# Sparse attention: ScalarE takes the next exponentials and the output copy ahead of a stored gate's silu, and the weight split after it

## The reference, cut to what matters

```python
logits = jnp.einsum('bqcgd,bqncd->bqcgn', qb, k_sel).astype(jnp.float32)
logits = logits + bias.astype(jnp.float32)
logits = jnp.where(valid[:, :, None, None, :], logits, -1e30)
p = jax.nn.softmax(logits, axis=-1).astype(v.dtype)
o = jnp.einsum('bqcgn,bqncd->bqcgd', p, v_sel)
...
o = o.transpose(1, 0, 2, 3).reshape(B, L, DSA_HEADS * DSA_HD)
return o * jax.nn.silu(z)
```

## Time and profile before

| | |
|---|---|
| median of 3 runs | 2004.09 us (2001.27 to 2006.61) |
| the profiled execution | 2000.59 us, of which span 1998.7 us |
| TensorE busy | 1961.4 us (98% of the span) |
| VectorE busy | 1144.5 us (57%) |
| ScalarE busy | 934.5 us (47%) |
| mean granted TensorE clock | 0.996 |

### The profile page before, as it was taken

The page is one execution under the profiler, slowest core; times in us unless marked ns, Lnnn a source line. Parts: engine busy times, 40 slices in busy tenths (PEclk is TensorE's granted clock), DMA queues, the critical chain, the costliest instruction groups (busy, mean ns, idle before and its releaser), DMA issues.

```text
span 1998.7 us, 32809 instructions
## 1 busy us (share of the span) xinstructions
PE 1961.4 (98%) x13488; PEld 1774.0 (89%) x13488; DVE 1144.5 (57%) x1595; ACT 934.5 (47%) x1647; POOL 151.8 (8%) x149
## 2 busy tenths in 40 slices
PE   8999999999999999999999999999999999999998
PEld 6798888878889778888999899999988798999998
DVE  3366357465343233353354999972277659999623
ACT  4443141455333342255454665552258846556522
POOL 0000000000000000000000333300000003333000
PEclk9999999999999999999999999999999999999999
DMA  6521122211234132332111233332331113322332
GB/s 178 147 85 64 43 85 88 81 64 64 106 127 148 63 108 103 109 113 102 67 60 69 84 118 106 107 117 95 106 116 43 64 64 114 109 107 106 110 111 76
DMA packets 29824, 191.24 MB, mean 96 GB/s; under 512 B 3689, under 2 KB 4841, under 8 KB 8562
## 3 DMA queue, kind: packets, MB, share of 16 engines
q1 hardware_dynamic: 26562, 178.58, 25.1%
q0 software_dynamic: 3120, 10.62, 2.0%
HBM read 185.38 MB, written 3.67 MB: 95 GB/s over the span
## 4 chain that ended last, share of the span: by engine, by line
PE 90%; DVE 4%; ACT 4%; issue 1%; DMA 0%; SPq 0%; DVEq 0%; ACTq 0%
PE PS L553 20%; PE PS L555 20%; PE PS L554 20%; PE PS L1026 7%; PE PS L1028 6%; PE PS L1027 6%; ACT whi L1533 1%; PE PS L887 1%; PE PS L706 1%; PE PS L723 1%; PE PS L1139 1%; PE PS L1354 1%; PE PS L909 1%; ACT hhi L1533 1%; PE PS L1331 1%
## 5 line engine op out<-in xcount | busy, mean ns | idle before, releaser
L2304 DVE TENSOR_TENSOR wlo<-raw,whi 128x2048 fp32r<-128x2048 f32 (+2 forms) x117 | 264.9, 2264 | 372.2 <-ACT whi L1533 371.8
L1533 ACT ACTIVATE whi<-raw 128x2048 fp32r<-128x2048 f32 (+2 forms) x250 | 312.5, 1256 | 211.7 <-PE PS L555 190.0
L553 PE MATMUL PS<-hhi,whi 128*128 128x512 f32 (+1 forms) x768 | 312.4, 407 | 3.2 <-DVE hlo L2351 3.2
L555 PE MATMUL PS<-hhi,wlo 128*128 128x512 f32 (+1 forms) x768 | 302.9, 394 | 0.0
L554 PE MATMUL PS<-hlo,whi 128*128 128x512 f32 (+1 forms) x768 | 301.1, 392 | 0.0
L553 PE MATMUL PS<-whi,ahi 128*128 128x256 f32 x704 | 194.3, 276 | 0.0
L554 PE MATMUL PS<-wlo,ahi 128*128 128x256 f32 x704 | 194.3, 276 | 0.0
L555 PE MATMUL PS<-whi,alo 128*128 128x256 f32 x704 | 194.3, 276 | 0.0
L1026 PE MATMUL PS<-shi,whi 128*128 128x256 f32 x640 | 179.6, 281 | 2.5 <-DVE a L2722 1.6
L553 PEld LDWEIGHTS PS<-hhi,whi 128*128 128x128 f32 (+1 forms) x768 | 144.3, 188 | 41.5 <-DVE hlo L2351 5.6
L1027 PE MATMUL PS<-slo,whi 128*128 128x256 f32 x640 | 178.6, 279 | 0.0
(11 more groups left out here) (458 smaller groups left out, 4603.5 us busy)
## 6 DMA issues: line engine op xcount, KB each, us to landing
raw<-in_stream SPq DMA_DIRECT2D x165, 1024.0 KB, 4.8
gpost<-in_gposts POOLq DMA_DIRECT2D x5, 512.0 KB, 7.6
X<-in_x SPq DMA_DIRECT2D x4, 512.0 KB, 6.8
X<-in_x POOLq DMA_DIRECT2D x1, 2048.0 KB, 11.5
out<-X SPq DMA_DIRECT2D x4, 512.0 KB, 2.6
bias_line<-linet POOLq DMA_DIRECT2D x1, 1536.0 KB, 35.3
tbias<-bias_line POOLq DMA_DIRECT2D x1, 1024.0 KB, 8.2
memx<-in_mem POOLq DMA_DIRECT2D x1, 1024.0 KB, 5.3
```

Of the source, the lines that this page charges most:

```text
L553: nc.tensor.matmul(out, lh, rh, start=(k == 0), stop=False)
L555: return nc.tensor.matmul(out, ll, rh, start=False, stop=(k == n_k - 1))
L1533: return nc.scalar.activation(out_, in_, func, scale=scale)
L2304: V_.tensor_tensor(wlo[:, s % 2, :, cols_], raw[:, s % 2, :, cols_], whi[:, s % 2, :, cols_], ALU.subtract)\
```

## The change

In the units that store a gate (4, 8, 12, 14) ScalarE's order after `turned(u)` was: silu of the gate, exponentials of `u + 1`, weight split, output copy of `u`. It becomes: exponentials of `u + 1`, output copy of `u`, silu, weight split. The other units keep their order, and the other engines' programs stay as they are.

```diff
                 elif u in (2, 6, 10):
                     store_features(dq, (u + 2) // 4, DSA_HD ** -0.5, splits=False)
-                elif u % 2 == 0:
-                    z_store(splits=False)
                 if u + 1 < 4 * NT:
                     exps(u + 1)
+                if u in (4, 8, 12, 14):
+                    output(u)
+                    z_store(splits=False)
+                    split(n + 1)
+                    continue
                 if u % 2 == 0:
                     split(n + 1)
```

## The result

The changed kernel takes 2011.68 us (median of 20 runs) against 2002.65 us for the kernel before (20 runs): ratio 1.0047, 95% interval 1.0036 to 1.0059. By that ratio it is +9.4 us, between +7.2 and +11.8 (the medians lie 9.0 apart); forecast were +9.5 and slower. The profiled execution of the changed kernel took 2005.82 us, near the low end of its 20 runs (2005.04 to 2019.63).

A forecast was written before the change was run, and what follows sets the result against it. TensorE bounds the attention stage, so only its waits or clock count: waits 5.07 − 0.30 = +4.8 us plus clock falls 4.7 us give +9.5 us, on 2004.09 us 2013.6 us; range 2007 to 2017 us.

The forecast's parts named there:

- The bound and the place: Attention stage: TensorE bounds it, so only its waits, chiefly at `turn(5)`, `turn(9)` and `turn(13)`, or its clock count.
- Exponentials and copy first: ScalarE, unit 4: exponentials start at 401.62, copy ends at 403.01 us; a gain of 0.71 if nothing else is late.
- Silu third: Units 4, 8, 12: silu 4.03 us later delays VectorE's product and division; `turn(5)` 1.69 us later, 5.07 over three units.
- The table switch: ScalarE before the silu: table load 1.28 us by the trace; the skill's drain would add 1.38 us per stall.
- Split last: ScalarE's weight split starts at 405.3 in place of 403.62 us, lower weights later: hidden by over 4 us.
- The cover of `turn(6)`: Division of unit 6 before `turn(6)`: 0.86 us to spare, 0.3 of it goes, cover holds.
- Unit 14: No product before the division there; `turn(15)` no longer waits: −0.30 us, at worst given back.
- The clock: TensorE's clock falls behind each of the three stalls, 1.6 us per fall; 0 to 4.7 us, 4.7 taken.
- Sum: Whole kernel: waits +4.8 us plus clock 4.7 us make +9.5 us, 2013.6 us.
- C: Rival: the output copy's early end counts and the division is ready in time, −2.4 us, 2001.7 us; chance 0.07.
- D: Rival: longer stalls, `turn(6)` cover fails or table switch costs more, +13 to +16, 2017 to 2020 us; chance 0.08.
- B: Rival: same stalls, clock falls once or not at all, +4.8 to +6.4, 2008.9 to 2010.5 us; chance 0.22.

The follow-up runs named there:

- e1: The changed kernel with VectorE's gate product of units 4, 8 and 12 written behind the next unit's division: 2003.03 us, ratio 1.0007 to the kernel before.
- e2: The kernel before with only the weight split moved behind the output copy in units 4, 8, 12 and 14, silu still first: 1998.64 us, ratio 0.9978.
- e3: The changed kernel with nine added 512-column matmuls on TensorE ahead of `turn` in units 5, 9 and 13: 2007.44 us, ratio 1.0031.
- e6: The changed kernel with eight added 512-column matmuls on TensorE ahead of `turn` in units 5, 9 and 13: 2009.50 us, ratio 1.0029.
- e5: The changed kernel run again with nothing altered (6 runs): 2013.03 us, ratio 1.0049 to the kernel before.

## Why the prediction was right

- *The bound and the place*: right. The time went into three waits of TensorE in the stage, and into nothing on the other engines as such.
- *Exponentials and copy first*: right to 0.1 us. With 1.37 added, the exponentials start at 401.62 (forecast 401.62) and the copy ends at 403.04 (403.01).
- *Silu third*: right. It ends at 405.38 (405.34), the multiply at 407.51 (407.48), `turn(5)` starts at 407.56 (407.62). Each wait grew by 1.63 us, forecast 1.69. That it is the product's place in VectorE's queue is shown by e1: when the product is moved behind the division, the waits of units 5, 9 and 13 go.
- *The table switch*: by the trace. The silu starts 0.01 us behind its load, as forecast from the row; the further 1.38 us of drain that "ScalarE: Activation LUTs" of the Trainium skill adds in "What ACT_TABLE_LOAD costs" does not show here either.
- *Split last*: right that it is hidden, shown by e1, where it is as late as in the changed kernel and `turn(5)` does not wait; in e2 the split behind the copy even wins. The cover of `turn(6)`, forecast as 0.86 less 0.3, held: in the changed kernel the division of unit 6 ends at 413.46 and `turn(6)` starts at 414.38, which leaves 0.78 beside the 0.14.
- *Unit 14*: right. `turn(15)` now follows its slot's matmul at once, and the 0.30 us are won:

```profile
498.24 0.40 PE L555 MATMUL PS<-hhi,wlo 128*128 128x512 f32 x1
498.48 1.03 PE L898 MATMUL PS<-K,lg 128*128 128x128 f32 x8
```

- *The clock*: right in mechanism, and in size within the forecast's own two cases: two falls in one execution, three in the other. By e3 and e6 each costs about 1.7 us (3.3 / 2 and 5.0 / 3), forecast 1.6. I had taken three. That these falls cost time is shown by e3 and e6 in the stage.
- *Sum*: +9.5 forecast, +9.4 (7.2 to 11.8) measured. With two or three falls the stage gives +8.0 or +9.8 (the measured +8.3 and +10.1, less 0.3 at unit 15), inside that interval. So closely to the middle it was also luck, since single runs of either kernel spread over 10 us and more. The time itself, forecast as 2013.6 us, came out 1.9 us lower: over 20 runs the kernel before has a median of 2002.65, and I had started from 2004.09 of three.
- *The rivals*: C (division ready in time) fell, since the division did not pass the product that waited. D fell, since no wait came at `turn(6)` and the table load took its 1.28 us. B (one fall or none) was seen in neither execution, but two executions are few.

## What to carry to other kernels

Before you move a producer later on one engine, look at what its consumer stands ahead of on another: the consumer's queue is in order, and here an instruction that nobody needed soon held up one that TensorE needed at once. Judge such a reordering edit by edit: moving the split last won time, moving the silu behind the exponentials lost more, because it gave up an idle stretch of ScalarE in which table load and silu were free. And price a stall of TensorE with the clock: where a fall followed, a stall that grew by 1.63 us cost about 3.3.

## What the runs showed of the hardware

- The waits of 2.2 us in the attention stage were followed by a fall of the clock to its lower level, 1.2 GHz, in five of six cases (three waits in each of two executions of the changed kernel); three of 1.3 to 1.4 us (e1) in none, the stage there reading 1.00 throughout. The length does not decide it alone: in the kernel before, a wait of 1.44 us elsewhere was followed by a stretch that reads 0.70. Adding matmuls whose result nobody reads, in the waits of 2.2 us, made the stage 3.3 to 5.0 us shorter.
- The falls are not fixed to a program. In the first execution of the changed kernel 244 to 248 us read 1.00, in e5, the same kernel, 0.50, with the same instructions at work (first and second row):

```profile
244.00:248.00 4.00, 4.00 (x35) 3.93 (x35) 0.00 (x0) 0.31 (x1) 0.00 (x0) 1.00 0.00 0
```

```profile
244.00:248.00 4.00, 4.00 (x21) 4.00 (x21) 0.00 (x0) 0.00 (x0) 0.00 (x0) 0.50 0.00 0
```

  Of the 20 runs of the changed kernel, those with a mean clock of 0.992 took 2012.1 to 2019.6 us, and those with 0.995 to 0.997 took 2005.0 to 2010.1 us; in between, at 0.993 and 0.994, they range over 2005.4 to 2018.0 us. So a good part of the spread between runs goes with the clock, which is why the stage's own row told more than the whole time.
